# Two tiles' expert results read through ScalarE's queue, two scalings in halves, and moved filler matmuls, in a two-block transformer kernel

## The reference, cut to what matters

```python
xn2 = modulate(rms_norm(h, g_norm_ffn[l]), sh2, sc2)
y = hier_moe(xn2, ...)            # 32 experts: silu(x @ gate) * (x @ up) @ down
h = h + gt2 * y                   # two expert rows per token, weighed and added
...
return rms_norm(h, g_final)       # after the second layer
```

```python
h = rmsnorm(x, pre_mix_g)
z = h @ w_in                      # 15 pieces of 512 columns, "v" and "dv0" first
...                               # linear attention, short convolution, dilated attention
x = x + rmsnorm(merged @ w_mix_out, post_mix_g)
h = rmsnorm(x, pre_ffn_g)
gt = causal_dwconv(h @ w_ff_gate, ff_conv_w) + ff_conv_b
y = (gelu(gt) * (h @ w_ff_up)) @ w_ff_down
x = x + rmsnorm(y, post_ffn_g)
```

## Time and profile before

| | us |
|---|---|
| median of 3 runs | 2712.83 (2712.51 to 2713.69) |
| the profiled execution | 2711.01 |
| its span in the profile | 2709.2 |
| TensorE matmuls busy | 2491.1 (92%) |
| VectorE, ScalarE, GpSimd busy | 778.6, 458.9, 170.0 |
| mean granted clock of TensorE | 0.988 |

### The profile page before, as it was taken

One profiled execution on the slowest core, in us unless ns is written; L12 is line 12 of the kernel. 1 busy time (PEld: TensorE's weight loads), 2 busy tenths in 40 slices (PEclk: granted clock), 3 DMA queues, 4 the chain that ended last, 5 costly groups with the idle time before them and its releaser, 6 DMA issues.

```text
span 2709.2 us, 30402 instructions
## 1 busy us (share of the span) xinstructions
PE 2491.1 (92%) x12192; PEld 1518.7 (56%) x12192; DVE 778.6 (29%) x1656; ACT 458.9 (17%) x1043; POOL 170.0 (6%) x193
## 2 busy tenths in 40 slices
PE   8999999999987778799999998777879999999998
PEld 3444554445554444345678655444445788886873
DVE  2694444115311111154253321000003323212210
ACT  2121223101100000022132110000102122102320
POOL 0000000000211111000000011111100000000000
PEclk9999999999999998999999999999999999999999
DMA  8464011425999999944424699999993332344331
GB/s 327 173 238 179 31 63 51 167 93 233 420 424 426 425 426 424 415 175 197 182 87 187 237 419 422 424 425 426 424 407 152 149 124 94 140 151 157 147 141 56
DMA packets 63047, 666.42 MB, mean 246 GB/s; under 512 B 13058, under 2 KB 13346, under 8 KB 24400
## 3 DMA queue, kind: packets, MB, share of 16 engines
q1 hardware_dynamic: 48672, 636.78, 57.5%
q0 software_dynamic: 13392, 24.82, 2.5%
q10 hardware_dynamic: 864, 3.15, 0.3%
HBM read 664.28 MB, written 21.02 MB: 253 GB/s over the span
## 4 chain that ended last, share of the span: by engine, by line
PE 74%; DMA 20%; SPq 2%; issue 2%; DVE 1%; ACT 1%; POOL 0%; DVEq 0%; ACTq 0%; POOLq 0%
PE act_bank L735 7%; DMA ring<-in_w_moe 7%; PE act_bank L722 7%; PE act_bank L857 6%; DMA xT<-in_w_moe 5%; PE act_bank L1297 5%; PE score_bank L1157 5%; PE vec_bank L873 4%; PE vec_bank L1169 4%; PE vec_bank L1040 4%; PE score_bank L857 4%; PE vec_bank L857 3%; PE act_bank L1534 3%; PE vec_bank L1534 3%; PE vec_bank L1552 3%; DMA heads<-in_w_moe 3%
## 5 line engine op out<-in xcount | busy, mean ns | idle before, releaser
L735 PE MATMUL act_bank<-xT,ring 128*128 128x512 f32 (+1 forms) x512 | 193.6, 539 | 0.0
L722 PE MATMUL act_bank<-ring,xT 128*128 128x512 f32 x416 | 183.4, 597 | 2.1 <-DVE xT L2161 1.6
L2599 DVE TENSOR_TENSOR heads<-work,vec_bank 128x256 f32<-128x256 f32 x64 | 27.0, 421 | 499.8 <-PE vec_bank L1157 499.8
L857 PE MATMUL act_bank<-xT,ring 128*128 128x256 f32 (+1 forms) x576 | 157.7, 427 | 1.9 <-issue 1.5
L735 PEld LDWEIGHTS act_bank<-xT,ring 128*128 128x128 f32 x512 | 97.0, 190 | 94.6 <-issue 91.4
L1157 PE MATMUL score_bank<-ring,branches 128*64 128x256 f32 x1024 | 122.3, 393 | 24.0 <-issue 12.4
L1157 PE MATMUL vec_bank<-ring,branches 128*64 128x256 f32 x1024 | 118.7, 384 | 27.7 <-DMA ring<-in_w_moe 27.7
L1169 PE MATMUL vec_bank<-ring,heads 128*64 128x512 f32 x512 | 116.9, 598 | 26.9 <-DMA ring<-in_w_moe 17.4
L857 PEld LDWEIGHTS act_bank<-xT,ring 128*128 128x128 f32 x576 | 109.2, 190 | 44.1 <-issue 32.0
L722 PEld LDWEIGHTS act_bank<-ring,xT 128*128 128x128 f32 x416 | 78.5, 191 | 97.7 <-issue 97.7
L1297 PE MATMUL act_bank<-xT,ring 128*128 128x256 f32 x576 | 126.6, 380 | 0.6 <-ACT work L1965 0.6
(11 more groups left out here) (423 smaller groups left out, 3353.3 us busy)
## 6 DMA issues: line engine op xcount, KB each, us to landing
ring<-in_w_moe SPq DMA_DIRECT2D x96, 2048.0 KB
ring<-in_w_in SPq DMA_DIRECT2D x29, 2048.0 KB
ring<-in_w_merge SPq DMA_DIRECT2D x27, 2048.0 KB
branches<-in_w_moe SPq DMA_DIRECT2D x24, 2048.0 KB
heads<-in_w_moe SPq DMA_DIRECT2D x24, 2048.0 KB
ring<-in_w_ada SPq DMA_DIRECT2D x23, 2048.0 KB
xT<-in_w_moe SPq DMA_DIRECT2D x22, 2048.0 KB
values<-in_w_moe SPq DMA_DIRECT2D x22, 2048.0 KB
```

The costliest lines, as they stand in the source:

```text
L722: mm = pe.matmul(b.t[:, :], xT[:, k, tile * P:(tile + 1) * P], w[:, k * COLS:(k + 1) * COLS], start=(k == 0), stop=(k == KD - 1))
L735: mm = pe.matmul(b.t[:, 0:n], w[:, k * COLS + f * P:k * COLS + (f + 1) * P], xT[:, k, 0:n], start=(k == 0), stop=(k == KD - 1))
L857: mm = pe.matmul(g.t[:, 0:n], merge_tile(l, i, MERGE_TILES * d + k), xs[:, k, 0:n], start=(k == 0), stop=(k == KD - 1))
```

## The change

The changes fall in three groups. First, the reads of results. Tile 0's read is issued by ScalarE ahead of the last expert's silu, tile 1's by ScalarE behind the last expert's copies, in both layers. SyncE keeps only tiles 2 and 3 of layer 0, behind V and VA. Second, two scalings are written as two instructions of 512 columns, with a semaphore `xhat_half` for the first, so that the first group of transposes waits only for that one. Third, fillers and copies move: 8 fillers ahead of block two's first transposes become 3, 3 are added between the last transposes and the feed-forward's loop, and VectorE's copies of tile 0 (`turned_mixed(0)`) go behind the first weighed half of tile 1 instead of ahead of the second.

```diff
...
@@ -1266,8 +1267,8 @@
 
-            pe.wait_ge(xhat_done.sem, NT * DEPTH + tile + 1)
             for q, b in enumerate((S[tile], V[2 + tile])):
+                pe.wait_ge(*((xhat_done.sem, NT * DEPTH + tile + 1) if q else (xhat_half.sem, tile + 1)))
                 pe.wait_ge(b.free, b.fills)
@@ -1277,8 +1278,8 @@
 
-            pe.wait_ge(xhat_done.sem, NT * DEPTH + 2 + tile + 1)
             for q, b in enumerate((S[tile], V[tile])):
+                pe.wait_ge(*((xhat_done.sem, NT * DEPTH + 2 + tile + 1) if q else (xhat_half.sem, 2 + tile + 1)))
                 pe.wait_ge(b.free, b.fills)
@@ -1319,7 +1320,7 @@
             last_sum(DEPTH - 1, 1)
-            keep_going(8)
+            keep_going(3)
             norm2_tile(0)
@@ -1596,6 +1597,7 @@
         turn_mixed(1)
+        keep_going(3, A[1])
         emptied(S[0], S[1], V[0], V[1])
@@ -1887,9 +1889,28 @@
 
+            def first_result():
+
+                y2 = y_rows[l].rearrange("(t k) n -> t (k n)", k=2)
+                for b in range(2):
+                    act.wait_ge(scattered[b], 16 * (N_EXP // 2 - 1) * (l + 1))
+                act.wait_ge(zeroed, 16 * KEPT_EXP * (l + 1))
+                act.wait_ge(V[3].full, base["V"][3] + (N_EXP - KEPT_EXP) // 2)
+                act.dma_start(y_tile[0], y2[0:P, :]).then_inc(y_in[0], 16)
+
+            def second_result():
+
+                y2 = y_rows[l].rearrange("(t k) n -> t (k n)", k=2)
+                act.wait_ge(*mark["last_gate", l])
+                act.dma_start(y_tile[1], y2[P:2 * P, :]).then_inc(y_in[1], 16)
+
             def turn(first, last):
                 for q in range(MOE_AHEAD):
+                    if last and q == MOE_AHEAD - 1:
+                        first_result()
                     expert(q % 2, first and q == 0, last and q == MOE_AHEAD - 1)
+                if last:
+                    second_result()
 
@@ -2744,7 +2765,9 @@
                 power(STT(out=r2, in0=sq_b[:, 2 + tile:3 + tile], scalar=1.0 / D, in1=r2, op0=ALU.mult, op1=ALU.add))
-                TS(x2first[:, tile, :], x2first[:, tile, :], r2, None, ALU.mult).then_inc(xhat_done.sem, xhat_done.up())
+                for c, done in enumerate((xhat_half, xhat_done)):
+                    half = slice(c * COLS, (c + 1) * COLS)
+                    TS(x2first[:, tile, half], x2first[:, tile, half], r2, None, ALU.mult).then_inc(done.sem, done.up())
                 b = V[2 + tile]
@@ -2961,10 +2984,10 @@
             def weighed(c):
-                if c == 1 and between is not None:
-                    between()
                 STT(out=y2[:, tile, c * 512:(c + 1) * 512], in0=banks[c].t[:, :], scalar=scale,
                     in1=gain[:, c * 512:(c + 1) * 512], op0=ALU.mult, op1=ALU.mult).then_inc(banks[c].free, banks[c].read())
+                if c == 0 and between is not None:
+                    between()
 
@@ -2988,8 +3011,10 @@
                 square_sum(tile, 2 + tile, lambda c: None)
-                TS(x2hat[:, tile, :], h[:, tile, :], rstd[:, 2 + tile:3 + tile], None, ALU.mult)\
-                    .then_inc(xhat_done.sem, xhat_done.up())
+                for c, done in enumerate((xhat_half, xhat_done)):
+                    half = slice(c * COLS, (c + 1) * COLS)
+                    TS(x2hat[:, tile, half], h[:, tile, half], rstd[:, 2 + tile:3 + tile], None, ALU.mult)\
+                        .then_inc(done.sem, done.up())
             turned_mixed(1)
@@ -3327,24 +3352,21 @@
             y2 = y_rows[l].rearrange("(t k) n -> t (k n)", k=2)
-            if tile == 0:
+            if tile == 2:
                 for b in range(2):
                     sp.wait_ge(scattered[b], 16 * (N_EXP // 2 - 1) * (l + 1))
                 sp.wait_ge(zeroed, 16 * KEPT_EXP * (l + 1))
-                sp.wait_ge(*last_read(max(c for c, s in AT.items() if c[:2] == ("expert", l) and s[0] == NSLOT)))
-            if tile == 1:
                 sp.wait_ge(*mark["last_gate", l])
             if tile == NT - 1:
                 sp.wait_ge(*mark["last_read", l])
             sp.dma_start(y_tile[tile], y2[tile * P:(tile + 1) * P, :]).then_inc(y_in[tile], 16)
 
-        results_behind = {("in", 1, "U"): ((0, 0),), ("in", 1, "VA"): tuple((0, tile) for tile in range(1, NT)),
-                          ("in2", 2, IN2_ORDER[0]): ((1, 0),), ("in2", 2, IN2_ORDER[1]): ((1, 1),)}
+        result_behind = {("in", 1, "V"): (0, 2), ("in", 1, "VA"): (0, 3)}
 
         def load_dense(c):
             load(c)
-            for at in results_behind.get(c, ()):
-                result(*at)
+            if c in result_behind:
+                result(*result_behind[c])
 
```

More of the change, by code:

```diff
@@ L528, in emit @@
     final_done = count("final_done")
+    xhat_half = count("xhat_half")
     alow_exp_in, alow_exp_out = count("alow_exp_in"), count("alow_exp_out")
```

## The result

| | before | now |
|---|---|---|
| median, us | 2712.67 (2711.77 to 2713.69, 4 runs) | 2691.97 (2691.51 to 2692.58, 4 runs) |
| profiled execution, its span | 2711.01, 2709.2 | 2691.51, 2689.7 |
| mean granted clock | 0.988 | 0.993 |

The ratio is 0.9924, 95% interval 0.9907 to 0.9941: 20.7 us faster by the medians, 16 to 25 us by the interval, where 23 were forecast (2690.0). The page's chain by engine has lost SyncE's 2% (against the earlier trace rows; it is 2% in the second profile of the kernel before too).

What follows compares the result with a forecast made beforehand. TensorE holds 74%; the winnable part is its short waits, chiefly for result reads queued behind weights. 8.8 + 6.35 + 1.0 + 3.4 + 3.4 = 23.0 us off 2712.83 gives 2689.8, say 2690; range 2686 to 2694, with rivals 2685 to 2700.

Steps and rivals of the forecast that it cites:

- Layer 0: End of layer 0's experts: earlier read starts the sum 6.4 us earlier, held clock adds 1.0 and 1.4; 8.8 together.
- hold-up of the weights: Both expert ends: the read's 1 MB delays expert 31's weights, 1.5 us in layer 0, 1.2 in layer 1.
- Layer 1: End of layer 1's experts: earlier read starts the sum 6.35 us earlier, and the held clock gives 1.0.
- part 2: Second block's start: three fillers instead of eight and halved scaling let the transposes start 3.4 us earlier.
- Part 3: Feed-forward's norm: copies moved 1.0 us, scaling in halves 0.5, clock held by fillers and shorter gap 1.9; 3.4 together.
- Cover for tile 1: Second tile's read lands by about 1151, covered by 10.54 us of dense products; up to 3 us of lateness free.
- Rivals. 1: Both expert ends: the read doesn't overtake, only goes out earlier; 9.3 us gained in all, 2703.5; chance 10%.
- Rivals 2 and 3: 2: clock falls in remaining gaps, 2696.2, 13%. 3: expert 31's weights held up 4.2 us at both ends, 2695.5, 6%.
- Rival 4: Both expert ends: ScalarE held issuing the read, delaying expert 31's silu; slower from about 20 us, 2723 at 25; 3%.

Runs made afterwards that it cites:

- e1: Changed kernel with only both result reads on ScalarE kept; eight fillers, whole scalings, old copies, no loop fillers as before: 2695.97 us, ratio to before 0.9935.
- e6: Changed kernel with eight filler products again instead of three ahead of the second block: 2693.59 us, ratio to before 0.9927.
- e9: Changed kernel with tile 0's copies back behind the second weighed half: 2694.10 us, ratio to before 0.9925.
- e7: Changed kernel with both scalings whole again, at the second block's norm and the feed-forward's: 2692.10 us, ratio to before 0.9922.
- e5: Changed kernel without the three filler products ahead of the feed-forward's loop: 2692.02 us, ratio to before 0.9919.
- e4: Changed kernel with tile 1's read back on SyncE behind the dense blocks, tile 0's still on ScalarE: 2699.55 us, ratio to before 0.9949.
- e3: Changed kernel with no read on ScalarE: SyncE issues tile 0's ahead of the first dense block, tile 1's behind the dense blocks: 2703.53 us, ratio to before 0.9959.

## Why the prediction held, point by point

**Layer 0, 8.8 forecast.** A gives 8.43. The reads alone give it (e1). The sum's last four matmuls start at about 1144.8 (half of the row at 1143.75), 19.85 us behind the copy at 1124.94, against 26.08 before: 6.2 for the 6.4. The hold-up of the weights was 1.43, forecast 1.5, but at the gate and up products, where I had put the larger part at the down product. The read landed after 8.5 us, not 12; with 6.4 us to spare nothing hangs on that here. In layer 1 it took 11.2 of the 12.4 us that it had.

**Layer 1 and part 2, 6.35 + 1.0 + 3.4 forecast.** The sum's last four matmuls start 17.6 us behind the start of expert 30's down product (half of the row at 2024.66), against 24.0 before: 6.4 for the 6.35. The hold-up is 1.0 (from that down product to the next 13.0 us, 12.0 before), forecast 1.2, and here too it lies at the up product's weights. C gives 10.79, the forecast 10.75. That match is partly luck: before again has a C of 34.78, since there the clock came back sooner behind the first sum, so against it the gain is 9.15. e6 shows what the five fillers cost once the clock holds: 1.3. The other 2 of part 2's 3.4 I put down to the clock, and so to the reads; that is argued, no run separates it.

**Part 3, 3.4 forecast.** D gives 3.02 against the first profile, 4.07 against the second. Copies 1.03 (e9), forecast 1.0; half 0.27 (e7), forecast 0.5; clock 1.7 to 2.8 where it falls, forecast 1.9. The mechanism of the last was wrong in one point: I gave the saved clock to the fillers and the shorter gap together. In one execution each, either was enough (e5, e9), and without both it fell in three of four.

**Cover for tile 1.** Costed at nothing with "up to 3 us of lateness free". e4 shows what is behind that nothing: 6.1 us in layer 0 if it stays with SyncE; in e3, where tile 0 is late as well, 0.6 in B and 4.5 behind it, through GpSimd's loads, which the prediction hadn't looked at. A term of zero, but one that the gain rests on.

**The sum.** The stretches add to 22.2 us (22.1 against the second profile); the forecast was 23.0, the medians moved by 20.7. The stretches are one execution each, and what lies ahead of them isn't still: expert 30's down product began anywhere from 1121.8 to 1128.6 in the fourteen profiles, through code that all share. The two profiles of before are the two earliest, which is why the profiled spans differ by 19.5 us and not 22.2. The forecast was taken from the median, so this doesn't explain it. Of its surplus of 2.3 us over the medians 0.8 is in the stretches; the other 1.5 stays open, and lies within the interval of 16 to 25 us.

**Rivals.** 1 fell: the read overtook, and e3 measures the overtaking. The view of the transfers in the 8.5 us of layer 0's read (queue, packets, MB, share of the 16 engines) has both queues moving side by side; q1 is SyncE's, q10 ScalarE's, and the 1.05 MB are the read:

```profile
q1 hardware_dynamic: 497, 2.22, 68.0%
q10 hardware_dynamic: 144, 1.05, 29.4%
```

In layer 1, where it took 11.2 us, SyncE's queue moved 3.39 MB beside it; in e1's layer 1, 2.12 MB and 8.5 us.

The Trainium skill, DMA: Bandwidth & Descriptors, Rules for kernel authors, has it that spreading transfers over engines for bandwidth doesn't help and saves only issue time. For bandwidth nothing here speaks against it (424 GB/s now, some 425 before). For the landing it does: here the issue moved from 2.8 us behind the copy at 1122.09 to 0.02, and the landing from 22.6 behind it to 8.5: of 14 us, 2.8 are issue time. The Trainium skill's section Queues, rings and completion order on the same page (engines take turns between queues, packet by packet) is what the runs agree with: both queues moved in the same 8.5 us.

Rivals 2 and 3 fell as wholes, yet their place was right in part: at expert 31's gate product hold-up and clock fell together in three profiles, at 1.4 us. Rival 4 fell: 0.34 us per issue. That SyncE's 13.32 us came from a full queue is a reading of the prediction's; the rows show only the length of the issue.

## What to carry to other kernels

A result that is needed at once shouldn't be read through the queue that carries bulk weights, even if it is issued first among equals: put it on a queue of its own, as early as its producer allows, and look at what its bytes hold up. Price an idle gap of the matrix engine with the products behind it, at both clocks, and when two short gaps follow each other, closing one may be enough. Profile a kernel twice before a single gap or a single fall of the clock is made a cause, and before two profiled spans are subtracted, see how far the stage's start lies apart in them.

## What the runs showed of the hardware that I had not expected

- On one queue, 1 MB behind an expert's pieces took 17.4 us (e3); on another queue, issued at the same point and beside the same traffic, 8.5. I had estimated 12. For it the last expert's down product came 1.4 us later.
- The clock's fall isn't fixed by the gaps alone. With gaps of 1.65 and 1.6 us it fell in three of four executions. In layer 1 expert 30's up product waits 2.9 us in every profile; in all but e1 and e3 it then took 5.0 to 5.4 us, in those two 3.67. That fall costs little: the next expert's weights come no sooner, and the faster ones waited 1.60 and 0.95 us for them (below, e1). From this product's start to the next gate product's it is 10.58 us in e1 and 10.45 in the changed kernel, 9.92 in e3 and 10.21 and 10.44 in the two profiles of before.

```profile
2002.43 3.67 PE L1158 MATMUL vec_bank<-ring,branches 128*64 128x256 f32 x32 [2.92 <-DMA ring<-in_w_moe]
...
2013.01 3.67 PE L1158 MATMUL score_bank<-heads,branches 128*64 128x256 f32 x32 [1.60 <-issue]
```
